# Two transformer blocks in fp32: the first mixer's shift added under the transposes, the last eighth of each modulation row and attention's shift on TensorE, window sums on VectorE

## The reference

```python
mod = (jax.nn.silu(c) @ ada_w[l] + ada_b[l]).reshape(bsz, 6, dm)
h = rms_norm(x, norm1_g[l]) * (1.0 + scale_a) + shift_a
proj = h @ w_in[l]
mix = jnp.concatenate([y_m, y_p], axis=-1) @ w_out[l]      # mLSTM and pool_group of proj
x = x + gate_a * mix
h = rms_norm(x, norm2_g[l]) * (1.0 + scale_f) + shift_f
x = x + gate_f * hierarchical_moe(h, ...)                  # 32 experts, two per token
...
mod = c_act @ w_ada[i] + b_ada[i]                          # second block, six rows again
h = rms_norm_2(x, norm_mix[i]) * (1 + sc_m) + sh_m
y = fox_mixer(h, ...)
x = x + g_m * y
x = x + g_f * (square(relu((rms_norm_2(x, norm_mlp[i]) * (1 + sc_f) + sh_f) @ w_mlp_in)) @ w_mlp_out)
```

## Time and profile before

| | |
|---|---|
| median of three runs | 2528.94 us (2528.35 to 2531.69) |
| profiled execution, its own time | 2527.01 us |
| its span | 2525.4 us |
| mean granted TensorE clock | 0.985 |
| busy | PE 2397.0 (95%), DVE 1941.2 (77%), ACT 1350.1 (53%), POOL 652.1 (26%) |

### The profile page before, as it was taken

One profiled execution on the slowest core, in us unless ns is written; L12 is line 12 of the kernel. 1 busy time (PEld: TensorE's weight loads), 2 busy tenths in 40 slices (PEclk: granted clock), 3 DMA queues, 4 the chain that ended last, 5 costly groups with the idle time before them and its releaser, 6 DMA issues. The chain is left out here.

```text
span 2525.4 us, 33783 instructions
## 1 busy us (share of the span) xinstructions
PE 2397.0 (95%) x11886; PEld 1983.0 (79%) x11886; DVE 1941.2 (77%) x2467; ACT 1350.1 (53%) x1908; POOL 652.1 (26%) x523
## 2 busy tenths in 40 slices
PE   6898989989999999999799999999899999999999
PEld 3675768767888888887489999998688888878887
DVE  5888468778989898987788888788866666656786
ACT  2242233257787777776487676676524444443432
POOL 1005644243333333332721111011033333310000
PEclk9998999999999999999899999999999999999999
DMA  7677545769878799998721111111432344487774
GB/s 258 179 230 252 176 167 211 281 249 384 345 262 331 279 394 402 398 404 321 233 95 51 51 50 44 51 39 64 171 117 88 138 160 162 164 318 272 283 265 151
DMA packets 181171, 535.88 MB, mean 212 GB/s; under 512 B 17438, under 2 KB 77442, under 8 KB 167736
## 3 DMA queue, kind: packets, MB, share of 16 engines
q1 hardware_dynamic: 163756, 470.71, 51.3%
q0 software_dynamic: 12592, 45.63, 4.8%
q10 hardware_dynamic: 4700, 17.92, 1.8%
HBM read 443.90 MB, written 90.33 MB: 212 GB/s over the span
## 5 line engine op out<-in xcount | busy, mean ns | idle before, releaser
L1691 PE MATMUL psum<-w_high,block_hT_high 128*128 128x512 f32 x576 | 232.3, 403 | 9.9 <-DVE w_low L1313 7.8
L1313 DVE TENSOR_TENSOR w_low<-first_w_up,w_high 128x2048 fp32r<-128x2048 f32 x72 | 187.7, 2644 | 51.2 <-ACT w_high L1307 51.2
L1693 PE MATMUL psum<-w_high,block_hT_low 128*128 128x512 f32 x576 | 225.2, 391 | 0.0
L1692 PE MATMUL psum<-w_low,block_hT_high 128*128 128x512 f32 x576 | 224.8, 390 | 0.0
L1691 PE MATMUL psum<-w_qkv_high,fox_hT_high 128*128 128x384 f32 (+1 forms) x512 | 183.1, 358 | 8.6 <-DVE v_high_low L2575 3.5
L1691 PE MATMUL psum<-mix_hT_high,w_in_high 128*128 128x512 f32 x400 | 167.4, 418 | 22.3 <-DVE w_in_low L739 18.8
L1409 POOL TENSOR_TENSOR block_out<-block_out,late_rows 128x1024 f32<-128x1024 f32 x35 | 95.3, 2724 | 358.0 <-ACT block_out L1570 358.0
L1313 DVE TENSOR_TENSOR w_low<-first_w_gate,w_high 128x2048 fp32r<-128x2048 f32 x74 | 169.5, 2294 | 21.0 <-ACT w_high L1307 21.0
L1691 PE MATMUL psum<-w_mlp_out_high,hidden_part_high 128*128 128x512 f32 x448 | 174.5, 390 | 3.3 <-DVE hidden L3926 1.7
L1307 ACT ACTIVATE w_high<-first_w_gate 128x2048 fp32r<-128x2048 f32 x74 | 141.2, 1912 | 65.6 <-DMA first_w_gate<-in_w_expert_gate 62.4
L1692 PE MATMUL psum<-w_qkv_low,fox_hT_high 128*128 128x384 f32 (+1 forms) x512 | 175.1, 342 | 0.0
(11 more groups left out here) (499 smaller groups left out, 6801.0 us busy)
## 6 DMA issues: line engine op xcount, KB each, us to landing
first_w_gate<-in_w_expert_gate SPq DMA_DIRECT2D x32, 2048.0 KB, 9.9
first_w_up<-in_w_expert_up SPq DMA_DIRECT2D x32, 2048.0 KB, 10.5
first_w_down<-in_w_expert_down SPq DMA_DIRECT2D x31, 2048.0 KB, 10.7
w_mlp_out_quarters<-in_w_mlp_out SPq DMA_DIRECT2D x78, 512.0 KB, 6.9
hidden_part<-hidden_parts SPq DMA_DIRECT2D x54, 512.0 KB, 4.4
v_aug<-in_w_ada SPq DMA_DIRECT2D x48, 512.0 KB, 4.6
expert_rows<-block_out POOLq DMA_DIRECT2D x34, 512.0 KB
v_aug<-in_ada_w SPq DMA_DIRECT2D x32, 512.0 KB, 4.7
```

What stands on the lines that cost most here:

```text
L1313: dve.tensor_tensor(wl[:, par, half], raw[kind][:, half], wh[:, par, half].bitcast(F32), ALU.subtract).then_inc(s_wl, 1)
L1691: pe.matmul(out, sh, mh, start=start, stop=False)
L1692: pe.matmul(out, sh, ml, start=False, stop=False)
L1693: return pe.matmul(out, sl, mh, start=False, stop=stop)
```

## The change

Three parts. **One:** in the mixer the shift is no longer added on DVE. ACT copies it as one row; eight small matmuls with a one-column selector turn it into 8x128 (twice, at partitions 0 and 32), ACT rounds it to its high part and DVE takes the low part of the second copy. `picks` (ACT, from the identity) says which of the rows belongs to which bank column. `shifts(t)` adds it by two matmuls of 128x512 that open the bank, and the eight transposes are accumulated onto it. Turns 5, 6 and 7 are set inside product(0,0) and product(1,0); four `keep_busy` calls are left of eleven; `scaled` runs three tiles ahead; pieces 0 to 2 are done among the rows. **Two:** the eighth piece of each modulation row goes to a fourth buffer and is multiplied by its silu(c) column on PE (L1115, two fp32 matmuls more, four records), accumulated with the sum; DVE has 70 pieces. `last_piece(b)` on SP waits for sum b − 1. The window sums are DVE's, each behind the low part of its iteration (11 to 14); POOL's memset of the ones in `vaug` waits for the last sum. **Three:** attention's shift goes the same way: picks are made again in the moe phase (ACT), the shift comes as columns by two small DMAs into `late`, PE turns it, and `turn_rows` opens its banks with two shift matmuls; `shifted_rows` is gone, and of `keep_busy` 14 and 4 are left.

```diff
-        hrow, gain, shift = ucT[:, 0:2, :], ucT[:, 2, :], ucT[:, 3, :]
+        hrow, gain, shift = ucT[:, 0:2, :], ucT[:, 2, :], zrow[0:1, 1, :]
+        ones_at = sbuf(ctx, "shift_selector", [1, 32 + 2 * KT])
+        shift_parts = sbuf(ctx, "mix_shift_parts", [32 + KT, P], F32R)
...
+        DK = KT - 1
+        NP = DK * len(later)
+        quota = [7, 4, 3, 4, 3, 7] + [6] * (NT - 6)
         until = [min(NP, sum(quota[:n + 1])) for n in range(NT)]
-        summed_in = [max(2, next(n for n in range(NT) if until[n] >= KT * (b + 1)) + 1) for b in range(len(later))]
+        summed_in = [max(2, next(n for n in range(NT) if until[n] >= DK * (b + 1)) + 1) for b in range(len(later))]
...
+                def last_piece(b):
+                    l, q = later[b]
+                    if b == 0:
+                        sp.wait_ge(s_gain, 1)
+                    else:
+                        sp.wait_ge(s_ms, b)
...
+                        if sent % DK == 2 and sent > DK:
+                            last_piece(sent // DK - 1)
...
+                    if n + 1 < NT and until[n + 1] == NP and until[n] < NP:
+                        last_piece(len(later) - 1)
...
-                for g in range(HM):
-                    win = 2 << g
-                    pool.wait_ge(ev, place[first["p"] + g, 1])
-                    src = pp[:, g, :]
-                    for j in range(g + 1):
-                        dst = uT[:, 2 + j % 2, :]
-                        sh = 1 << j
-                        then(pool.tensor_tensor(dst[:, sh:], src[:, sh:], src[:, 0:S - sh], ALU.add))
-                        then(pool.tensor_copy(dst[:, 0:sh], src[:, 0:sh]))
-                        src = dst
-                    then(pool.tensor_tensor(src[:, 0:16], src[:, 0:16], fix[:, g, :], ALU.mult))
-                    then(pool.tensor_scalar(src, src, 1.0 / win, None, ALU.mult))
-                    pool.tensor_tensor(pp[:, g, :], src, pp[:, g, :], ALU.subtract).then_inc(p_sum, 1)
-                    pool.wait_ge(p_sum, g + 1)
-                    if g == 2:
-                        pool.wait_ge(s_ma, NP)
...
+                pool.wait_ge(s_ms, len(later))
+                pool.memset(vaug[:, :, :, P:P + 1], 1.0).then_inc(z, 1)
...
+                act.wait_ge(idm, 4)
+                for r, n in ((0, 32), (32, KT)):
+                    act.activation(picks[r:r + n, :].rearrange("p (k t) -> p k t", t=P), ident[r:r + n, r:r + KT].unsqueeze(2).to_broadcast([n, KT, P]), ACT.Copy)
...
+                act.activation(shift, psum[0:1, 0:2, :].rearrange("p b n -> p (b n)"), ACT.Copy).then_inc(s_shift, 1)
...
-                act.activation(shift, psum[:, 0:2, :].rearrange("p b n -> p (b n)"), ACT.Copy).then_inc(s_shift, 1)
...
-                    dve.wait_ge(s_sc, t + 1)
-                    dve.tensor_tensor(hrow[:, t % 2, :], hrow[:, t % 2, :], shift, ALU.add).then_inc(s_h, 1)
...
+                def window_sums(g):
+                    win = 2 << g
...
+                    src = pp[:, g, :]
...
+                        dve.tensor_copy(dst[:, 0:sh], src[:, 0:sh])
+                        then(dve.tensor_tensor(dst[:, sh:], src[:, sh:], src[:, 0:S - sh], ALU.add))
+                        src = dst
+                    then(dve.tensor_tensor(src[:, 0:16], src[:, 0:16], fix[:, g, :], ALU.mult))
+                    dve.scalar_tensor_tensor(pp[:, g, :], src, 1.0 / win, pp[:, g, :], ALU.mult, ALU.subtract).then_inc(p_sum, 1)
+
...
-                dve.wait_ge(s_shift, 1)
                 scaled(0)
                 scaled(1)
-                low(1)
+                low(0)
+                dve.wait_ge(s_ch, 1)
+                dve.tensor_tensor(shift_parts[32:32 + KT, :], bank[0][32:32 + KT, 0:P], shift_parts[32:32 + KT, :].bitcast(F32), ALU.subtract).then_inc(s_cl, 1)
+                scaled(2)
                 for t in range(TT):
                     h_low(t)
-                    if t + 2 < TT:
-                        scaled(t + 2)
+                    if t + 3 < TT:
+                        scaled(t + 3)
+                    if t == 3:
+                        low(1)
+                    if t >= 4 and t < 7:
...
+                def shifts(t, start):
+                    for hf in range(2):
+                        ins = pe.matmul(bank[4 + 2 * (t % 2) + hf], shift_parts[:], picks[:, hf * HALF:(hf + 1) * HALF], start=start, stop=not start)
+                    return ins
+
...
+                    if t >= 1:
+                        shifts(t, True)
+                    pe.wait_ge(s_sc, t + 1)
                     for k in range(KT):
-                        ins = pe.transpose(turned(t)[:, k, :], hrow[:, t % 2, k:D:KT], ident[:])
+                        ins = pe.matmul(turned(t)[:, k, :], hrow[:, t % 2, k:D:KT], ident[:], start=t == 0 and k % 4 == 0, stop=t > 0 and k % 4 == 3, is_transpose=True)
+                    if t == 0:
+                        pe.wait_ge(s_cl, 1)
+                        ins = shifts(t, False)
                     ins.then_inc(s_tr, 1)
...
-                keep_busy(pe, bank[6], ident, 6)
+                keep_busy(pe, bank[6], ident, 2)
+                pe.wait_ge(s_sel, 3)
+                pe.wait_ge(s_shift, 1)
+                for k in range(KT):
+                    ins = pe.matmul(shift_sums, ones_at[:, KT - 1 - k:31 + 2 * KT - k], shift[:, k:D:KT], start=k == 0, stop=k == KT - 1)
+                ins.then_inc(s_ct, 1)
+                keep_busy(pe, bank[6], ident, 1)
                 turn(0)
-                pe.wait_ge(pc, 2)
-                keep_busy(pe, bank[6], ident, 2)
                 turn(1)
-                pe.wait_ge(s_hl, 1)
-                keep_busy(pe, bank[4], ident, 1)
+                keep_busy(pe, bank[1], ident, 1)
                 turn(2)
                 turn(3)
-                pe.wait_ge(s_shift, 1)
-                keep_busy(pe, bank[0], ident, 2)
+                turn(4)
                 pe.wait_ge(s_lo, 1)
                 pe.wait_ge(s_hl, 4)
-                product(0, 0)
-                turn(4)
+                product(0, 0, range(0, 2))
                 turn(5)
+                product(0, 0, range(2, 6))
+                turn(6)
+                product(0, 0, range(6, 8))
                 pe.wait_ge(s_lo, 2)
                 pe.wait_ge(s_gain, 1)
-                product(1, 0)
-                turn(6)
+                product(1, 0, range(0, 2))
                 turn(7)
+                product(1, 0, range(2, 8))
                 pe.wait_ge(s_hl, TT)
                 product(0, 1)
                 product(1, 1)
@@ -1056,11 +1107,15 @@
                             pool_product(2 * (n - NT + 3) + hf - 1)
...
-                            pe.wait_ge(s_ma, KT * (b + 1))
+                            pe.wait_ge(s_ml, 16 * b + 16)
...
+                            l, _ = later[b]
                             for hf in range(2):
-                                ins = pe.matmul(bank[6 + hf][0:1, :], ones[:, 0:1], acc[:, b % 2, hf * HALF:(hf + 1) * HALF], start=True, stop=True)
+                                pe.matmul(bank[6 + hf][0:1, :], csil[:, l, DK:KT], spare[:, 3, hf * HALF:(hf + 1) * HALF], start=True, stop=False)
+                            pe.wait_ge(s_ma, DK * (b + 1))
+                            for hf in range(2):
+                                ins = pe.matmul(bank[6 + hf][0:1, :], ones[:, 0:1], acc[:, b % 2, hf * HALF:(hf + 1) * HALF], start=False, stop=True)
...
+                    sp.wait_ge(t_cz, 5)
+                    for r in (0, 32):
+                        sp.dma_start(late[:, 6 * D + r:6 * D + r + KT], mods[6 + SHIFT_A:7 + SHIFT_A, :].rearrange("o (p k) -> (o p) k", k=KT)).then_inc(t_x1, 16)
...
+                            pe.matmul(bank[2 * (t % 2) + hf], shift_parts[:], picks[:, hf * HALF:(hf + 1) * HALF], start=True, stop=False)
+                        pe.wait_ge(s_xn, t + 1)
...
+                    pe.transpose(bank[6][0:32 + KT, 0:P], shift_cols, ident[:]).then_inc(s_ct, 1)
+                    keep_busy(pe, bank[7], ident, 14)
                     turn_rows(0)
-                    keep_busy(pe, bank[7], ident, 5)
+                    keep_busy(pe, bank[7], ident, 4)
                     project(0, range(0, 8))
...
-                    def shifted_rows(t):
-                        dve.wait_ge(s_xn, t + 1)
-                        dve.tensor_tensor(xr[t % 3], xr[t % 3], fshift, ALU.add).then_inc(s_sh, 1)
```

122 lines of the change are left out of this document (73 added, 49 removed).

## The result

| | before | changed |
|---|---|---|
| median of nine runs | 2535.13 us (2526.31 to 2536.39) | 2508.70 us (2503.16 to 2521.60) |
| profiled execution, its own time | 2527.01 us | 2508.33 us |
| its span | 2525.4 us | 2506.7 us |

The ratio is 0.9918, 95% interval 0.9904 to 0.9932: 17 to 24 us of 2528.94, 20.7 in the middle. In a later set of five runs of the changed kernel it was 0.9902 (0.9887 to 0.9918). The profiled executions stand 18.7 apart, against the 25.7 of the forecast; the one of the kernel before is a quick run of it (2527.01, where the nine have a median of 2535.13), so that what follows, read from two profiles, is rather short of the whole. The median lies within the forecast's range, 5.5 us above its number.

A forecast was written before the change was run, and what follows sets the result against it. PE, busy 95% of the span, bounds the kernel, waiting mostly for DVE's low weight parts. −11.8 + 0 − 13.4 − 0.5 = −25.7 gives 2501.3 from the profiled execution, 2503.2 for the median; range 2492 to 2519.

The forecast's parts named there:

- First rows: Mixer, 34.5 to 92.3 us: without DVE's shift adds, tile 2 starts at 80.5 rather than 92.35; −11.8 us.
- product(0,0) starts at 52.3: Mixer's first rows: DVE's new order ends h_low(3) at 52.2, so the first product starts at 52.3 rather than 56.84.
- rival B: Mixer's start: with fewer busy-keeping calls, two product halves run at 1.2 GHz; +7.5 us, so 2511; chance 0.12.
- The allowance of 2.0: Mixer's first rows: 2.0 us added for a start at the lower clock, making 78.6 into 80.6.
- Tiles 2 to 8: Mixer stretch of 96.5 us, PE-bound: 8.6 us of added PE work against lost waits and clock loss; ±0, bounds −4 and +6.
- Tiles 9 to 13: Mixer stretch of 89.2 us: DVE gets ahead, the waits for low weights go, PE takes 75.8 us; −13.4.
- the allowance of 3: Tiles 9 to 13: 3 us for the first tile, mostly a 0 to 4 stall behind the gate rows, and slower clock.
- Rival A: Tiles 9 to 13: the ring of piece loads still paces DVE, 2.3 us a piece; +11.5, so 2515; chance 0.22.
- the others stand in iterations with a low part and nothing else for PE: Tiles 9 to 13: of 20 us of window sums on DVE, only the first 2.9 stand before pieces.
- SP's queue: Mixer: eighth-piece loads wait for the row sum before, with later loads behind; tightest at tile 14, 0 up to +3 us.
- rival C: Mixer's ten rows: SP is held behind PE sums and the ring runs empty; +34 us, 2563; chance 0.05.
- Attention: Attention phase: eight adds leave DVE, PE gains 3.6 us of work; −0.5 us, bounds −3 and +2.

The follow-up runs named there:

- attention undone: The changed kernel with attention's part taken back (shift added on DVE, moe phase as before); ratio 0.9947 to the kernel before.
- The square of kernels: Kernels with neither, either or both of sums moved to DVE and eighth piece to PE; fifth to tenth sum: 85.96, 82.1, 81.9, and 76.3 to 78.4 us.
- changed again: The changed kernel itself, unaltered, timed again in a later set beside the kernel before; ratio 0.9902 (0.9887 to 0.9918).
- the pair that differs in nothing else: The kernel before, and the same with only attention's part put in; ratio 0.9995 (0.9979 to 1.0012), stretch 137.7 us against 139.9.

## Why the prediction was right, and where not

**First rows, −11.8 forecast, −8.0 measured.** The adds went and DVE did not pace the end, as worked out. The step that failed is "product(0,0) starts at 52.3", by way of the selector products and what stands around them, of which the prediction said only that it "takes the place of busy-keeping products". They take 3.88 us, and in nine of eleven profiles the clock is down or falls at turn 0 behind them. Turn 0 started at 41.35 rather than 40.8, and it and the four shift matmuls behind it, 1.05 and 1.20 us at the upper clock (attention undone), took 1.92 and 2.07. From turn 1's start to product(0,0) it is 9.4 us in each of the four profiles where the clock stayed up from turn 1 on. With turn 1 at 42.98, as with attention undone, that would give 52.4 (my estimate): the path was right, and nearly all of the 3.3 us missed is the clock's. DVE waited 4.34 us for PE there:

```profile
44.52 1.28 DVE L722 SCALAR_TENSOR_TENSOR ucT<-sigmoid_oT,x_stat,ucT 128x1024 f32<-128x1024 f32 x1 [4.34 <-PE psum L1008]
```

This is rival B's mechanism at another place. It spoke of the first products; it was the turns, one to three of them in each profile with calls (two in the first) and five with no calls at all. The page cited there, the Trainium skill's "TensorE: Matmul & The Clock Gate", section "Part 4: PE-mode transpose", agrees with the kernel without calls: five turns at the lower clock, and the upper one at the next turn, behind the first true products. It does not say all: in the four profiles just named the clock rose between turn 0 and turn 1. The allowance of 2.0 for the clock after product(0,0) was about right (28.7 us where 26.3 is the bare work; 27.2 to 30.3 in the others). By all eleven profiles tile 2 starts at 81.0 to 84.7, in the middle 82.9, so that the −8.0 of the first profile is near the low end.

**Tiles 2 to 8, ±0 forecast, +0.2.** PE is busy throughout, 87.0 us of old work and 8.6 of new, at clock 1.00. The 5.4 us of lower clock went and paid for part of it. This was the term's working.

**Tiles 9 to 13, −13.4 forecast, −12.9.** The square of kernels bears out both halves of the reasoning, seven to six pieces and no POOL beside it, some 4.5 us each. That the number fits to half a microsecond is luck in part: by the middle of the kernels with the old mixer (87.8) and of those with both halves (77.4) the stretch gives 10.4. Of the allowance of 3, the stall behind the gate rows was not there in the first profile (0.3 us of waits for low parts in all) and 2.1 us in "changed again"; 2 us went to eighth pieces (1.8 and 0.6) that I had put at nothing. Rival A had the right sign on its transfers (5.7 us to land, and 39 loads in the stretch rather than its 35) and the wrong conclusion.

**The v tiles, not a term, +4.6.** The step that failed: "the others stand in iterations with a low part and nothing else for PE". I priced the four window sums by DVE's load and asked who stands behind them on DVE, but not who waits for their result. ScalarE evicts tile 15 over the buffers that the sums use as scratch, and waits for all four. And the move set POOL free: its gated weights, which stood behind the sums on POOL, now ran beside the fourth. The 20 us estimated for the sums on DVE became some 25 (12.2 for the first three, as estimated, and 12.9 for the fourth, estimated at 7.1). Of the 4.6 us, 2.7 are PE's wait and the rest mostly the lower clock behind it, where eight transposes take 1.92 us rather than 1.04. The rule on the port that VectorE and GpSimd share, from the Trainium skill's "Perfetto Trace Analysis", section "Optimizing Scalar/DVE Operations", was weighed for the stretch that POOL left; these rows agree with it in the stretch that POOL went to.

**SP's queue, 0 to +3.** In "changed again" SP issued nothing from 232.6 to 241.1 us, held at the last eighth piece for the sum before it, and PE waited nowhere for the weights and pieces behind: rival C fell. What did cost is the other direction, an eighth piece landing behind the sum that wants it.

**Attention, −0.5.** −2 in the profiles of the pair that differs in nothing else, within its bounds (−3 to +2), but 7 to 11 us by the ratios of three kernels, outside them, and so open; "PE waits once for one, 1.68" was an undercount. Over that row PE waited for shifted rows four times, 9.7 us.

**The sum.** −25.7 less the two failed steps: +3.8 in the first rows, +4.6 at the v tiles, −2.1 more behind them, and 0.7 in the others, is −18.7. That is the account of two profiles. The ratios say 20.7 (17 to 24) and 24.8 (21 to 29): the 25.7 lies above the first interval and inside the second.

## What to carry to other kernels

When work moves to an engine with time to spare, ask three things of it: who waits for its result, what buffers it holds while it is late, and what the engine that it leaves will now do at the same time. Here the last made a sum of 6.7 us one of 12.9, and one wait, holding the other engine back, undid it to a hundredth in that stretch, though the gain in the whole is too small for these runs to show. Two remedies for one wait (fewer pieces, faster pieces) are best measured as a square, and the square needs more than one profile a corner: by single profiles the two seemed to give more together (9.6) than the sum of each (8.0), and the repeats took that back.
